# Norms of heads and of the convolution: roots by token and a spread by TensorE, with a new order of conversions and attention

## The reference, cut to what matters

```python
o = gla_chunked(...)                                        # 4 heads, 256 values each
o = o * lax.rsqrt(jnp.mean(o * o, axis=-1, keepdims=True) + EPS)
o = o * head_g ; o_gla = o * silu(g_gate)

u = causal_depthwise_conv(a * sigmoid(g), conv_w, conv_b)   # 31 taps, 512 channels
mu = jnp.mean(u, -1) ; var = jnp.mean(jnp.square(u - mu), -1)
y = silu((u - mu) * lax.rsqrt(var + EPS) * ln_w + ln_b) * silu(z)

o = w @ v                                                   # 4 heads, 128 values each
o = rmsnorm(o, subln_w) * (1.0 - lambda_init) * silu(z)
x = x + concat(y_ssd, y_cfm, y_att) @ w_out
```

## Time and profile before

| | |
|---|---|
| median of 3 runs | 3558.71 us (3557.51 to 3559.10) |
| the profiled execution | 3561.85 us |
| its span, first to last instruction | 3560.1 us |
| mean granted TensorE clock | 0.978 of full speed |
| TensorE busy | 3393.7 us, 95% |
| VectorE busy | 2129.8 us, 60% |
| ScalarE busy | 1263.6 us, 35% |

### The profile page before, as it was taken

One profiled execution on the slowest core, in us unless ns is written; L12 is line 12 of the kernel. 1 busy time (PEld: TensorE's weight loads), 2 busy tenths in 40 slices (PEclk: granted clock), 3 DMA queues, 4 the chain that ended last, 5 costly groups with the idle time before them and its releaser, 6 DMA issues.

```text
span 3560.1 us, 42715 instructions
## 1 busy us (share of the span) xinstructions
PE 3393.7 (95%) x15682; PEld 2726.4 (77%) x15682; DVE 2129.8 (60%) x3132; ACT 1263.6 (35%) x1967; POOL 149.8 (4%) x100
## 2 busy tenths in 40 slices
PE   8999999999999999999989998898999999889899
PEld 7887887877787888788878876686777887667677
DVE  5565666776655545434244775666755576565774
ACT  4333334454332233323152224324433223432442
POOL 2000000000010000000050000000002000000000
PEclk9999999999999999999999999998999999999899
DMA  5333336576755555555443443344445343335445
GB/s 172 129 110 119 131 111 201 186 255 226 269 189 178 172 180 186 193 175 209 145 145 114 166 139 102 129 158 146 154 167 206 108 169 124 116 131 166 143 150 201
DMA packets 293231, 575.62 MB, mean 162 GB/s; under 512 B 63392, under 2 KB 107168, under 8 KB 293024
## 3 DMA queue, kind: packets, MB, share of 16 engines
q1 hardware_dynamic: 293024, 572.90, 48.1%
HBM read 440.66 MB, written 132.12 MB: 161 GB/s over the span
## 4 chain that ended last, share of the span: by engine, by line
PE 54%; issue 24%; DVE 11%; ACT 5%; DMA 2%; DVEq 2%; POOLq 1%; SPq 0%; ACTq 0%
PE bank L552 36%; PE bank L551 11%; DVE weights_low L476 3%; ACT weights_high L403 2%; POOLq L462 1%; DVE arena L2002 1%; ACT arena L1937 1%; DMA convert_in<-mix 1%; DVE residual_in L2077 1%; DVEq L2581 1%; PE bank L1090 1%; DVE arena L1997 1%; PE bank L728 1%; ACT arena L1934 1%; DMA convert_in<-x 1%
## 5 line engine op out<-in xcount | busy, mean ns | idle before, releaser
L552 PE MATMUL bank<-act_high,weights_high 128*128 128x512 f32 x3584 | 1452.0, 405 | 90.4 <-DVE stream_out L489 38.0
L552 PE MATMUL bank<-act_low,weights_high 128*128 128x512 f32 x3584 | 1421.3, 397 | 0.0
L476 DVE TENSOR_TENSOR weights_low<-weights_raw,weights_high 128x1024 fp32r<-128x1024 f32 x528 | 658.2, 1247 | 1069.8 <-ACT weights_high L403 1067.9
L403 ACT ACTIVATE weights_high<-weights_raw 128x1024 fp32r<-128x1024 f32 x528 | 558.3, 1057 | 1486.6 <-PE bank L552 1250.8
L552 PE MATMUL bank<-act_high,weights_low 128*128 128x512 f32 x3584 | 963.4, 389 | 0.0
L552 PEld LDWEIGHTS bank<-act_high,weights_high 128*128 128x128 f32 x3584 | 689.5, 192 | 259.7 <-issue 66.0
L552 PEld LDWEIGHTS bank<-act_low,weights_high 128*128 128x128 f32 x3584 | 689.4, 192 | 141.5 <-issue 2.9
L552 PEld LDWEIGHTS bank<-act_high,weights_low 128*128 128x128 f32 x3584 | 672.8, 188 | 140.2
L551 PE MATMUL bank<-weights_high,act_high 128*128 128x512 f32 x640 | 256.6, 401 | 18.9 <-DVE stream_out L489 14.8
L551 PE MATMUL bank<-weights_high,act_low 128*128 128x512 f32 x640 | 251.8, 394 | 0.0
L2077 DVE SCALAR_TENSOR_TENSOR residual_in<-residual_in,arena 128x512 f32<-128x512 f32 x240 | 180.4, 752 | 20.1 <-issue 0.9
(11 more groups left out here) (325 smaller groups left out, 2737.7 us busy)
## 6 DMA issues: line engine op xcount, KB each, us to landing
weights_raw<-in_w_all SPq DMA_DIRECT2D x528, 512.0 KB, 3.4
convert_in<-mix SPq DMA_DIRECT2D x80, 256.0 KB, 4.2
fm_b<-stream_out SPq DMA_DIRECT2D x72, 256.0 KB, 2.3
mix<-arena SPq DMA_DIRECT2D x64, 256.0 KB, 2.7
x_part<-stream_out SPq DMA_DIRECT2D x48, 256.0 KB, 4.1
residual_in<-x_part SPq DMA_DIRECT2D x48, 256.0 KB, 5.0
x<-stream_out SPq DMA_DIRECT2D x48, 256.0 KB, 4.8
convert_in<-x SPq DMA_DIRECT2D x48, 256.0 KB, 4.0
```

What stands on the lines that cost most here:

```text
L403: e.activation(WH[:, t % 3, :], RAW[:, t % 3, :], ACT.Copy).then_inc(wh_ready, 1)
L476: e.tensor_tensor(WL[:, t % 3, :], RAW[:, t % 3, :], WH[:, t % 3, :].bitcast(F32), ALU.subtract).then_inc(wl_ready, 1)
L552: return e.matmul(bank[s][:, :], a[:, s * P:(s + 1) * P], h, start=start, stop=stop)
```

## The change

Norms (gla heads, the convolution's norm, attention heads): the sum of squares is taken as one moving column of ones for each block of 128 tokens (4 columns, over two tiles in gla, 4 for each of four tiles in the convolution, which VectorE then adds), the scaling, root and reciprocal run on 128x4 (`gl_st`, `cf_st`, `at_st`), a copy spreads them (`spread`), and TensorE multiplies by the identity (`cast`) into the bank that held the sums; what multiplies by the norm now reads that bank. In gla and attention the gate is multiplied by the norm first. Slots: attention starts two slots sooner (`ATT_START` 87 + 6h, `att_pre` 82), `cfm_norm` one (86), the convolution gives up slots 85 and 86 and its blocks 2 and 3 take nine slots with five taps to a step; the conversions of tiles 0 to 11 stand in slots 89 to 100, one to a slot; those of the heads' tiles follow the heads, two slots sooner (100, 106, 112, 118).

```diff
-ATT_START = [89 + 6 * h for h in range(4)]
+ATT_START = [87 + 6 * h for h in range(4)]
...
-            put(B[l] + (90 + k // 2 if k < 8 else 96 + (k - 8) // 2), 6 + 2 * l, k)
+            put(B[l] + 89 + k, 6 + 2 * l, k)
...
# gla_pe
-                    e.wait_ge(*gl_d[o].at("mean", u))
+                    e.wait_ge(*gl_d[o].at("mix1", u))
...
-            for a in range(2):
-                e.wait_ge(*a_.at(f"square{a}", t))
-                mm = e.matmul(mid[0][:, :], ONES[:, :], gl_sq[:, a, :], start=a == 0, stop=a == 1)
+            e.wait_ge(*a_.at("square1", t))
+            for b in range(TB):
+                for a in range(2):
+                    mm = e.matmul(mid[0][:, b:b + 1], gl_sq[:, a, b * P:(b + 1) * P], ONES[:, 0:1], start=a == 0, stop=a == 1)
             mm.then_inc(*p.mark("sum"))
             yield
             yield
+            e.wait_ge(*d.at("spread", t))
+            for b in range(TB):
+                mm = e.matmul(mid[0][:, b * P:(b + 1) * P], gl_m[:, b * P:(b + 1) * P], IDENT[:, :], start=True, stop=True)
+            mm.then_inc(*p.mark("cast"))
             yield
             yield
...
# gla_act
-            e.activation(gl_m, gl_m, ACT.Sqrt).then_inc(*a_.mark("root"))
+            e.activation(gl_st, gl_st, ACT.Sqrt).then_inc(*a_.mark("root"))
...
# gla_dve
             e.wait_ge(*p.at("sum", t))
-            e.tensor_scalar(gl_m, mid[0][:, :], 1.0 / 256, EPS, ALU.mult, ALU.add).then_inc(*d.mark("mean"))
+            e.tensor_scalar(gl_st, mid[0][:, 0:TB], 1.0 / 256, EPS, ALU.mult, ALU.add).then_inc(*d.mark("mean"))
             e.wait_ge(*a_.at("root", t))
-            e.reciprocal(gl_m, gl_m)
-            yield
-            e.drain()
-            for a in range(2):
-                e.scalar_tensor_tensor(gl_sq[:, a, :], mid[2 + a][:, :], gl_hb[:, n, a + 1:a + 2], gl_m, ALU.mult, ALU.mult)
-            e.drain()
+            e.reciprocal(gl_st, gl_st)
+            e.drain()
+            e.tensor_copy(gl_m.rearrange("p (b n) -> p b n", b=TB),
+                          gl_st.rearrange("p (b o) -> p b o", o=1).broadcast_to([P, TB, P])).then_inc(*d.mark("spread"))
+            yield
+            e.wait_ge(*p.at("cast", t))
             e.wait_ge(gl_gin, 32 * (h + 1))
             for a in range(2):
-                e.tensor_tensor(gl_sq[:, a, :], gl_sq[:, a, :], gl_gate[:, a, :], ALU.mult).then_inc(*d.mark(f"mix{a}"))
+                e.tensor_tensor(gl_gate[:, a, :], mid[0][:, :], gl_gate[:, a, :], ALU.mult)
+            e.drain()
+            for a in range(2):
+                e.scalar_tensor_tensor(gl_sq[:, a, :], mid[2 + a][:, :], gl_hb[:, n, a + 1:a + 2], gl_gate[:, a, :],
+                                       ALU.mult, ALU.mult).then_inc(*d.mark(f"mix{a}"))
...
# the convolution's norm: the same, cast in step 3, read in step 4
-        CFM_TAPS = [range(4 * n, min(4 * n + 4, TAPS)) for n in range(8)]
+        CFM_TAPS = [[range(n, min(n + w, TAPS)) for n in range(0, TAPS, w)] for w in (4, 4, 5, 5)]
...
-                mm = e.matmul(mid[1][:, :], ONES[:, :], cf_sq[:, k % 2, :], start=k == 0, stop=k == 3)
+                for b in range(TB):
+                    mm = e.matmul(mid[1][:, k * TB + b:k * TB + b + 1], cf_sq[:, k % 2, b * P:(b + 1) * P], ONES[:, 0:1],
+                                  start=True, stop=True)
...
+            e.tensor_reduce(cf_st, mid[1][:, 0:4 * TB].rearrange("p (k b) -> p b k", b=TB), AX, add)
...
# attention: the same, sum in step 8, spread and cast in step 9, read in step 10
-            e.wait_ge(*(at_d[o].at("mix", u) if h else cf_d.at("var", l)))
+            e.wait_ge(*(at_d[o].at("mix", u) if h else cf_d.at("t3", l)))
...
-            free = [at0 + t for t in [*range(17, 25), *range(29, 33), *range(37, 41), *range(45, 48), *range(66, 87)]]
+            free = [at0 + t for t in [*range(17, 25), *range(29, 33), *range(37, 41), *range(45, 48), *range(66, 85)]]
...
-                stage(f"cfm_conv{l}_{i}", free[10 * i:10 * i + 10], sp=lambda e, l=l, i=i: cfm_conv_sp(e, l, i),
+                stage(f"cfm_conv{l}_{i}", free[[0, 10, 20, 29][i]:[10, 20, 29, 38][i]], sp=lambda e, l=l, i=i: cfm_conv_sp(e, l, i),
...
-            stage(f"att_pre{l}", place(at0 + 84, 3), sp=lambda e, l=l: att_pre_sp(e, l), act=lambda e, l=l: att_pre_act(e, l),
+            stage(f"att_pre{l}", place(at0 + 82, 3), sp=lambda e, l=l: att_pre_sp(e, l), act=lambda e, l=l: att_pre_act(e, l),
...
-            stage(f"cfm_norm{l}", place(at0 + 87, 7), sp=lambda e, l=l: cfm_norm_sp(e, l), pe=lambda e, l=l: cfm_norm_pe(e, l),
+            stage(f"cfm_norm{l}", place(at0 + 86, 7), sp=lambda e, l=l: cfm_norm_sp(e, l), pe=lambda e, l=l: cfm_norm_pe(e, l),
```

More of the change, by code:

```diff
@@ L1012, in build @@
         gl_mx = [sem(f"gl_mix{a}") for a in range(2)]
-        gl_p = [steps(f"gl_pe{n}", "alpha s7 s0 s1 s2 s3 s4 s5 s6 far0 far1 out sum") for n in range(2)]
+        gl_p = [steps(f"gl_pe{n}", "alpha s7 s0 s1 s2 s3 s4 s5 s6 far0 far1 out sum cast") for n in range(2)]
         gl_a = [steps(f"gl_act{n}", "ln f0 f1 f2 f3 f4 f5 f6 f7 f8 far0 far1 square0 square1 root") for n in range(2)]
         gl_d = [steps(f"gl_dve{n}", "min d0 d1 g0 d2 g1 m7 d3 g2 m0 d4 g3 m1 d5 g4 m2 d6 g5 m3 d7 g6 m4 d8 g7 m5 g8 m6 "
-                                    "mean mix0 mix1") for n in range(2)]
+                                    "mean spread mix0 mix1") for n in range(2)]
         A = Arena(MID_AB, MID_AB + GLA_N)
@@ L2066, in cfm_conv_dve @@
             u, w = cf_u[i % 2], CFW[l][:, i, :]
-            for taps in CFM_TAPS:
+            for taps in CFM_TAPS[i]:
                 for k in taps:
@@ L2320, in att_pe @@
             e.wait_ge(*a_.at("squarev", t))
-            e.matmul(mid[1][:, :], ONES[:, :], at_sq, start=True, stop=True).then_inc(*p.mark("sum"))
+            for b in range(TB):
+                mm = e.matmul(mid[1][:, b:b + 1], at_sq[:, b * P:(b + 1) * P], ONES[:, 0:1], start=True, stop=True)
+            mm.then_inc(*p.mark("sum"))
             yield
+            e.wait_ge(*d.at("spread", t))
+            for b in range(TB):
+                mm = e.matmul(mid[1][:, b * P:(b + 1) * P], at_m[:, b * P:(b + 1) * P], IDENT[:, :], start=True, stop=True)
+            mm.then_inc(*p.mark("cast"))
             yield
```

51 lines of the change are left out of this document (31 added, 20 removed).

## The result

| | before | after |
|---|---|---|
| median of 10 runs | 3559.15 us (3551.91 to 3562.45) | 3567.97 us (3563.91 to 3569.22) |
| ratio | | 1.0024, 95% interval 1.0014 to 1.0034 |
| the profiled execution's span | 3560.1 us | 3566.7 us |
| mean granted TensorE clock | 0.978 | 0.979 |
| VectorE busy | 2129.8 us | 2084.7 us |

What follows compares the result with a forecast made beforehand. TensorE's queue, its work and waits, was taken as the bound (busy 95%). Terms: gla +1.8, taps +7.2, attention -12.6, clock +6.8 and +3.4, sum +6.6 us; forecast median 3565 us, range 3549 to 3577.

Steps and rivals of the forecast that it cites:

- The three terms: gla heads +1.8 us; slots 72 and 80 with clock +14.0; convolution's norm, attention and output slots with clock -9.2.
- Matmuls: TensorE's added small products: +1.0 us per gla head, attention head and convolution's norm, 14 us if nothing hides it.
- A norm on VectorE: Each of 14 norms falls to about 1.2 us on VectorE, about 3.6 us less each, 50 us in all.
- gla: Four gla heads: head 0 costs 0, head 1 at slot 47 -0.2, heads 2 and 3 +1.0 each; sum +1.8 us.
- Taps: Five taps a slot delay bank copies at slots 72 and 80: +7.2 us over two layers, plus 6.8 of clock.
- Attention: Slots 88 onward, layers 2 and 3: shorter waits for VectorE, less added matmuls, -12.6 us; clock at slot 96 +3.4.
- my own sign: Forecast is wrong if TensorE's waits in a layer's slots 88 to 102 sum under 8 us, or clock holds at 72 and 80.
- The clock falls after the new sums: Rival, chance 0.12: one-column runs in gla and the convolution's norm lower TensorE's clock, 1.7 us each; 3569 to 3576 us.
- The clock holds: Rival, chance 0.18: waits at slots 72 and 80 stay short enough to keep TensorE's clock; 3555 to 3558 us.
- The count on which the clock's price stood: TensorE's waits of 2.5 us or more all had a fallen clock behind; of 14 at 1.5 to 2.3 us, three.
- VectorE clears attention: Rival, chance 0.20: VectorE runs ahead in attention, half the 13.5 us of waits a layer go; about 3548 us, or 3541.
- SP: Head 0's gate load waits in slot 96 for stores issued there, other loads behind it; costed at 0.

Runs made afterwards that it cites:

- both repairs: The changed kernel with five-tap slots moved off slots 71 and 79 and gla's product with the identity in step 16, not 17: 3543.09 us, ratio 0.9954.

## Why the prediction was right, and where it was not

**The sum.** Forecast +6.6 between profiled executions, measured +6.6 between spans and +8.8 between medians. The three terms came out at +1.8, +15.0 and -9.3 against +1.8, +14.0 and -9.2. That the total of the spans meets the forecast to 0.1 us is luck: slot 206 alone, where nothing was changed, differs by 4.8 us between these two executions, and other slots far from the change take it back.

**Matmuls: right.** Eight one-column products take 1.84 us (forecast 1.8), the four against the identity make a unit 0.93 us longer (0.9 to 1.0), the convolution's 16 take 3.7 us (3.75). The columns are no saving, as the rows of before said.

**A norm on VectorE: right.** 1.2 us were forecast for scaling, root, reciprocal and copy; VectorE's timeline of after, one gla head:

```profile
310.54 0.16 DVE L1272 TENSOR_SCALAR arena<-bank 128x4 f32<-128x4 f32 x1
310.97 0.18 DVE L1274 RECIPROCAL arena<-arena 128x4 f32<-128x4 f32 x1 [0.27 <-ACT arena L1174]
311.22 0.43 DVE L1276 COPY arena<-arena 128x512 f32<-128x512 f32 x1
```

From 310.54 to 311.65 are 1.1 us.

**gla: right in sum, short in the reading.** At slot 48 the wait fell from 5.5 to 4.2, where I had 5.3, and the slot by 0.3. That VectorE would wait in step 17 was in the text; that this wait was the change's own, and one `yield` from gone, was not.

**Taps: right.** Waits of 3.1 and 2.9 (forecast 2.9 and 2.75) in layer 2, 3.1 and 2.8 in layer 3: 7.8 us more against 7.2. The clock fell behind all four and cost 7.1 us against 6.8.

**Attention: right by the sum, wrong by its parts.** I had forecast 31.6 us of waits in the two layers' attention slots and 3.4 us of clock. After has 20.6 us of waits in slots 88 to 116 (13.8 in layer 2, 6.9 in layer 3) and a half clock over 23.9 us, which costs 11.9. That is 32.6 against 35.0: the waits were forecast 11 us too long, the clock's loss 8.5 too small. By layer the slots came out at -5.8 and -3.5 where the forecast has -6.7 and -2.5 (-8.4 and -4.2, with 1.7 of clock each), so two misses of 1 us cancel as well. By my own sign, under 8 us of waits in slots 88 to 102 of a layer, the step was wrong in layer 3. The sign was badly made: I had written that in slots 89 to 95 a slower TensorE only shortens its next wait, and then watched the waits alone. Both halves show in slots 89 and 90: the unit behind the convolution's sums ran at 0.84 and took 1.6 us longer (10.71, against 9.11 where the clock held), and the wait for the norm's cast, forecast at 2.1, was 0.3. Three traces with the same code in slots 89 to 98 of layer 2 bear it out in part. The changed kernel has 10.7 us of waits and 6.8 us at half clock there, both repairs 7.9 and 13.7, and they took 89.59 and 89.61 us: VectorE's chain sets the length, and clock and waits share what is left over. But the kernel with gla's cast moved has 9.6 and 20.5 and took 94.2 us: its slots 89 to 97 took 78.2 us, as in the changed kernel (78.1), but in slot 98 the clock fell (0.68 over 16.06 us, where the changed kernel has 11.47 at 1.00), and there no shorter wait gave the time back. Why it fell in one and not in the other is not shown, and such a fall is not in the forecast.

**The rivals.** "The clock falls after the new sums" happened, but only behind the convolution's 3.7 us and not behind any gla run of 1.8 us. The run of 1.8 us that spoke for it, at 1854.01 before, has a fallen clock in that trace alone; the same products left it at 1.00 in all thirteen others. Behind the convolution's sums the fall cost little by itself, since a wait for VectorE stood behind it. Slots 89 and 90 of layer 2 together took 18.0 us in the changed kernel (3.4 us at half clock), 19.1 with both repairs (6.8 us) and 19.7 in the kernel with gla's cast moved, where the clock held in slot 89, the norm's product with the identity then waited 1.9 us, and the clock fell behind that. "The clock holds" was wrong for the taps. The count on which the clock's price stood has an exception: TensorE's first wait before, 11.1 us for the first conversion, is longer than 2.5 us and has no fallen clock behind it. "VectorE clears attention" was half there: in layer 3 the waits were half of the forecast, and the clock took most of it back.

**SP: wrong.** The gate load was costed at 0, as VectorE gets to these slots later. ScalarE waited 5.62 us for the load behind it and VectorE 5.03 us in slot 97, and the logits of slot 98 in layer 2 waited 2.5 us for the gate (L2509), which I had not listed; with the load moved and both repairs the last 0.7 us of that wait went in layer 2.

**ScalarE's table.** The root in slot 96 follows silus and needs its table. ScalarE's timeline of after:

```profile
2483.22 1.28 ACT L2413 ACT_TABLE_LOAD   x1
2484.52 0.20 ACT L2413 ACTIVATE arena<-arena 128x4 f32<-128x4 f32 x1
```

The root starts 0.02 us after the load's end, and VectorE waits 0.57 us for it in place of 0.27: the switch costs 0.3 us here. The Trainium skill (ScalarE: Activation LUTs, "What ACT_TABLE_LOAD costs") adds about 1380 ns of drain to the load; this trace does not show it, and leaving it out was right.

**What the change lacked.** Its idea was sound: with the same slots and norms, taps and one product placed otherwise, it is 16.0 us faster than before in place of 8.8 slower. I saw the two places, priced the taps rightly and gla's head 1 at next to nothing, and took both as given.

## What to carry to other kernels

When work is squeezed out of slots, ask not how much each slot gets but which slot stands ahead of a wait of the bottleneck: a fifth tap of 0.83 us in each of the three or four slots up to a pass end cost about 4 us with its clock, and the same taps in the three slots behind it cost nothing that shows. A shorter step for an engine pays only if no new wait in the same step hands the time back; put the product that turns its result around in the step before its reader. And where two engines trade waits, forecast their sum with the clock's loss, not the list of waits.

## What was not expected of the hardware

The clock fell with no wait ahead of it: behind 3.68 us of products whose output has one column it was 0.84 over 10.71 us or 0.72 over 12.3 us. Eleven kernels here have these sums (one of them with 32 columns), in two layers each. The clock fell in the slot behind them in 21 of the 22 places. It stayed at 1.00 in one, layer 2 of the kernel with gla's cast moved, where the slot took 9.11 us and the clock fell one slot on, behind a wait of 1.9 us. Behind gla's runs of 1.84 us it did not fall. The kernel before, with four 128x512 sums in that place, kept 1.00 in both layers, as did the two kernels with the long norms and the new slots. Products of 32 columns did the same as those of one. Nor was the wait's length a sure sign: a wait of 2.5 us in slot 98 of layer 2 left the clock at 1.00 in the changed kernel, and one of 2.6 in the same place was followed by 0.68 over 16.06 us in the kernel with gla's cast moved. One of 2.1 us in slot 97 of layer 2 left it at 1.00 in the changed kernel and was followed by 0.84 over 10.80 us with both repairs. What decides between them stays open.
